# Output projection of block 1 ended by halves of the tokens, with the first half's norms beside it, and the norms' transposed tiles in four PSUM banks

## What is computed

```python
for l in range(DEPTH):
    h = rms_norm(x, mix_pre_gain[l])
    ... = split_columns(h @ w_in[l])
    ...                                   # 16 heads of four kinds of attention
    mixed = jnp.concatenate([o_a, o_b, o_c, o_d], axis=-1) @ w_out[l]
    x = x + rms_norm(mixed, mix_post_gain[l])
    h = rms_norm(x, ffn_pre_gain[l])
    y = conv_gated_mlp(h, w_up[l], conv_w[l], conv_b[l], w_down[l])
    x = x + rms_norm(y, ffn_post_gain[l])
```

## Time and profile before

| | us |
|---|---|
| median of three runs | 2374.84 |
| the profiled execution | 2370.15 |
| its span | 2368.4 |
| TensorE busy | 2066.8 |
| VectorE busy | 1739.2 |
| ScalarE busy | 841.7 |
| GpSimd busy | 698.6 |

### The profile page before, as it was taken

How to read it: one execution, slowest core, us unless ns; L and a number is a source line. 1 busy time by engine, 2 the same in 40 slices (tenths; PEclk the granted TensorE clock), 3 DMA queues, 4 the chain that set the end, 5 groups by cost and what they waited for, 6 DMA issues and landing times. The chain is left out here.

```text
span 2368.4 us, 27992 instructions
## 1 busy us (share of the span) xinstructions
PE 2066.8 (87%) x8693; PEld 1338.4 (57%) x8698; DVE 1739.2 (73%) x4197; ACT 841.7 (36%) x2074; POOL 698.6 (29%) x633
## 2 busy tenths in 40 slices
PE   7999999999979999998778788699899987777777
PEld 6779987779979775544233332297745543332222
DVE  6757777677767677778787877576677778787875
ACT  6656655666658611211111111277211211111110
POOL 1300001200001043444445434110343454444441
PEclk9999999999999889999989999999799999999999
DMA  6354532335545369999999999754499999999996
GB/s 221 110 179 179 186 136 83 135 125 186 186 145 164 125 236 419 420 421 421 422 421 421 421 421 421 272 158 152 167 420 419 422 421 421 421 421 421 421 421 270
DMA packets 138669, 700.53 MB, mean 296 GB/s; under 512 B 14392, under 2 KB 40248, under 8 KB 66872
## 3 DMA queue, kind: packets, MB, share of 16 engines
q0 software_dynamic: 73728, 536.90, 54.7%
q1 hardware_dynamic: 64824, 162.22, 19.6%
HBM read 698.03 MB, written 1.05 MB: 295 GB/s over the span
## 5 line engine op out<-in xcount | busy, mean ns | idle before, releaser
L2052 PE MATMUL bank<-ARENA 128*128 128x512 f32 x2048 | 989.8, 629 | 219.2 <-DVE ARENA L2354 217.8
L2052 PEld LDWEIGHTS bank<-ARENA 128*128 128x128 f32 x2048 | 385.1, 198 | 802.6 <-DVE ARENA L2354 431.7
L2344 DVE CUSTOM_DVE_ANT_0 ARENA<-ARENA 128x1024 f32<-128x1024 f32 x512 | 626.2, 1223 | 268.6 <-DMA ARENA<-in_uv_rows,ARENA 261.4
L1956 POOL DMA_INDIRECT ARENA<-in_uv_rows,ARENA x512 | 587.2, 1147 | 702.6 <-PE bank L2052 638.3
L154 PE MATMUL bank<-PARTS,PARTS 128*128 128x256 f32 (+4 forms) x1488 | 487.3, 327 | 12.6 <-DVE PARTS L284 5.9
L155 PE MATMUL bank<-PARTS,PARTS 128*128 128x256 f32 (+6 forms) x1552 | 496.3, 320 | 0.0
L156 PE MATMUL bank<-PARTS,PARTS 128*128 128x256 f32 (+6 forms) x1552 | 495.6, 319 | 0.0
L2160 ACT ACTIVATE ARENA<-ARENA 128x1 f32<-128x1 f32 x512 | 104.0, 203 | 1043.5 <-DVE ARENA L2344 1043.0
L155 PEld LDWEIGHTS bank<-PARTS,PARTS 128*128 128x128 f32 (+2 forms) x1552 | 297.8, 192 | 16.5 <-issue 1.0
L156 PEld LDWEIGHTS bank<-PARTS,PARTS 128*128 128x128 f32 (+2 forms) x1552 | 297.4, 192 | 16.8
L154 PEld LDWEIGHTS bank<-PARTS,PARTS 128*128 128x128 f32 x1488 | 285.9, 192 | 36.8 <-DVE PARTS L284 7.1
(11 more groups left out here) (262 smaller groups left out, 1900.3 us busy)
## 6 DMA issues: line engine op xcount, KB each, us to landing
ARENA<-in_w_up_tiles SPq DMA_DIRECT2D x44, 1024.0 KB, 6.7
ARENA<-in_w_down SPq DMA_DIRECT2D x44, 512.0 KB, 3.4
ARENA<-in_w_out SPq DMA_DIRECT2D x32, 512.0 KB, 4.2
ARENA<-in_wq_tiles SPq DMA_DIRECT2D x16, 1024.0 KB, 11.4
ARENA<-in_w_in SPq DMA_DIRECT2D x40, 384.0 KB, 3.8
ARENA<-in_w_in SPq DMA_DIRECT2D x24, 512.0 KB, 8.6
ARENA<-in_w_in SPq DMA_DIRECT2D x40, 256.0 KB, 2.8
ARENA<-in_uv_rows,ARENA POOLq DMA_INDIRECT x512
```

The source lines that it names most:

```text
L1956: nc.gpsimd.indirect_dma_start(out=slot[i % SLOTS], out_offset=None, in_=table[:, :], in_offset=bass.IndirectOffsetOnAxis(ap=picked[:, t, ...
L2052: last = mm(row_banks[t][n][:, :], diag[i % N_DIAG], slot[i % SLOTS][:, D + n * 512:D + (n + 1) * 512], start=(c == 0), stop=(c == NPICK - ...
L2344: v.tensor_tensor_reduce(u, u, xn[:, t, :], 1.0, 0.0, ALU.mult, ALU.add, dots[:, t, c:c + 1]).then_inc(S("dots_ready"), 1)
```

## The change

1. `post_norm` gets a mode `by_half`: its squares, gain products and roots can be issued one at a time, in the order of banks (0,0), (1,0), (0,1), (1,1), written as (t, n) with n the chunk; each waits for its own bank. VectorE takes a bank after ScalarE's square of it.

```diff
-            def act(act):
-                act.wait_ge(*done)
-                for t in range(NT):
...
+            order = [(t, n) for n in range(2) for t in range(NT)] if by_half else [(t, n) for t in range(NT) for n in range(2)]
+            squares_of = [order.index((t, 1)) + 1 for t in range(NT)]
+            def act(act, i):
+                t, n = order[i]
+                act.wait_ge(*done(t, n))
+                if n == 1 and not by_half:
+                    act.wait_ge(S(tag + "_scaled"), before + 2 * t + 1)
+                nc.scalar.activation(junk[:, 2 * t + n, :], out_bank[t][n][:, :], ACT.Square, scale=D ** -0.5,
+                                     accum_out=ss[:, 2 * t + n:2 * t + n + 1]).then_inc(S(tag + "_squares"), 1)
...
+            def scaled(dve, t, n):
+                if turn_waits(t, n):
+                    dve.wait_ge(*turn_waits(t, n))
+                cols = slice(n * 512, (n + 1) * 512)
+                nc.vector.tensor_tensor(mg[:, t, cols], out_bank[t][n][:, :], gain[:, cols], ALU.mult
+                                        ).then_inc(S(tag + "_scaled"), 1)
+            def turn_waits(t, n):
+                if by_half:
+                    return S(tag + "_squares"), before + order.index((t, n)) + 1
+                return (S(tag + "_squares"), before + 2 * t + 1) if n == 0 else done(t, n)
...
+                for t, n in ([(0, 0), (1, 0), (0, 1)] if by_half else [(0, 1), (0, 0), (1, 1), (1, 0)]):
+                    scaled(dve, t, n)
+            def dve_x(dve, t):
+                if by_half and t == 1:
+                    scaled(dve, 1, 1)
                 dve.drain()
-                for t in range(NT):
-                    dve.wait_ge(S(tag + "_rstd"), before_x + t + 1)
-                    nc.vector.scalar_tensor_tensor(X[:, t, :], mg[:, t, :], rstd[:, t:t + 1], X[:, t, :],
-                                                   ALU.mult, ALU.add).then_inc(S(tag + "_x"), 1)
```

```diff
+            def place(k):
+                return bank[4 + k // 4 * 2 + k % 2], k // 2 % 2 * T
...
+                    act.wait_ge(S(tag + "_turned"), before_k + ((2, 4, 4, 4)[k % 4] + k // 4 * 4))
+                    if k >= 2:
+                        act.wait_ge(S(tag + "_lo"), before_k + k - 1)
+                    to, at = place(k)
+                    nc.scalar.mul(HT_HI[:, k, :], to[:, at:at + T], gain(k)).then_inc(S(tag + "_hi"), 1)
...
+            def pe(pe, t):
+                pe.wait_ge(S(tag + "_xn"), before_t + t + 1)
+                for k in (0, 2, 1, 3, 4, 6, 5, 7):
+                    to, at = place(k)
+                    last = nc.tensor.transpose(to[:, at + t * P:at + (t + 1) * P], xn[:, t, k * P:(k + 1) * P], ident)
+                    if t == NT - 1:
+                        last.then_inc(S(tag + "_turned"), 1)
```

```diff
-                    return bank[4 + 2 * (c % 2) + t]
+                    return bank[t] if c == 0 else bank[4 + 2 * (c % 2) + t]
...
+                        if h >= NHD - 2:
+                            out.highs(act, KD + 2 * (h + 2 - NHD), KD + 2 * (h + 2 - NHD) + 2)
                     high_part(NHD // 2 - 1)
-                    out.highs(act, KD, out.n_units)
+                    out.highs(act, KD + 4, out.n_units)
...
-                            if n == KD:
-                                pe.wait_ge(s_("att_probsT"), NHD)
                             out.product(pe, n, out_bank)
+                    def projected_by_half():
+                        pe.wait_ge(s_("att_probsT"), NHD)
+                        for n in range(KD, out.n_units):
+                            last = out.half_product(pe, n, out_bank, 0)
+                        last.then_inc(s_("out_half"), 1)
+                        for n in range(KD, out.n_units):
+                            out.half_product(pe, n, out_bank, 1).then_inc(out.used(n)[0], 1)
...
-                            pe.wait_ge(S("norm_lo"), KD * 2 * l + max(2, k + 1))
+                            pe.wait_ge(S("norm_lo"), KD * 2 * l + k + 1)
```

4. The streams of `feeding(l)`:

```diff
+                projected = {(0, 0): out.used(KD), (1, 0): out.used(KD), (0, 1): mixed.out_half, (1, 1): out.done}
+                after_mix = post_norm(2 * l, lambda t, n: projected[t, n], out_bank, mix_post, f"mix_post_{l}", xn, junk,
+                                      by_half=True)
+                mid = pre_norm("norm", after_mix.x_ready, l, 1, xn, turn=2 * l + 1)
...
-                    after_ffn.pool(pool)
+                    for t in range(NT):
+                        after_mix.pool(pool, t)
+                        mid.pool(pool, t)
...
                 def act(act):
+                    for i in range(3):
+                        after_mix.act(act, i)
+                    mid.act_squares(act, 0)
                     up_down.act_early(act)
-                    after_mix.act(act)
-                    mid.act_squares(act)
+                    after_mix.act(act, 3)
+                    mid.act_squares(act, 1)
                     mid.act_high(act)
...
                 def dve(dve):
+                    after_mix.dve_scaled(dve)
+                    after_mix.dve_x(dve, 0)
+                    mid.dve_scale(dve, 0)
                     up_down.dve_early(dve)
-                    after_mix.dve(dve)
-                    mid.dve_scale(dve)
+                    after_mix.dve_x(dve, 1)
+                    mid.dve_scale(dve, 1)
                     mid.dve_low(dve)
                     up_down.dve(dve, following.lows if l + 1 < L else nothing)
...
                 def pe(pe):
                     up_down.pe_early(pe)
-                    keep_busy(32)
-                    mid.pe(pe)
+                    mid.pe(pe, 0)
+                    keep_busy(20, bank[0])
+                    mid.pe(pe, 1)
                     up_down.pe(pe)
                     if l + 1 < L:
                         keep_busy(32)
-                        pre.pe(pe)
+                        for t in range(NT):
+                            pre.pe(pe, t)
 
                 return stage(sp=sp, pool=pool, act=act, dve=dve, pe=pe)
```

More of the change, by code:

```diff
@@ L186, in stage, with keep_busy, post_norm @@
             return namedtuple("Stage", programs)(**programs)
-        def keep_busy(count):
+        def keep_busy(count, to=bank[7]):
             for _ in range(count):
-                nc.tensor.matmul(bank[7][:, :], ZERO[:, 0:P], ZERO[:, :], start=True, stop=True)
-        def post_norm(turn, done, out_bank, gain, gain_sem, mg, junk):
+                nc.tensor.matmul(to[:, :], ZERO[:, 0:P], ZERO[:, :], start=True, stop=True)
+        def post_norm(turn, done, out_bank, gain, gain_sem, mg, junk, by_half=False):
             tag = "post"
@@ L240, in read, with pre_norm @@
                 eng.wait_ge(S(tag + "_scaled"), before + 2 * NT)
-            return stage(act=act, pool=pool, dve=dve, banks_read=banks_read, read=read,
+            return stage(act=act, pool=pool, dve_scaled=dve_scaled, dve_x=dve_x, read=read,
                          x_ready=lambda t: (S(tag + "_x"), before_x + t + 1))
-        def pre_norm(tag, x_ready, l, which, xn, banks_read=None, first=4, turn=0):
+        def pre_norm(tag, x_ready, l, which, xn, turn=0):
             ss = STAT[:, 120:122]
@@ L1201, in _ @@
                     pool.drain()
-                    pre.pool(pool)
+                    for t in range(NT):
+                        pre.pool(pool, t)
                     for l in range(L):
@@ L1208, in _ @@
                 def _(act):
-                    pre.act_squares(act)
+                    for t in range(NT):
+                        pre.act_squares(act, t)
                     first.highs(act, 0, 6)
@@ L1220, in _ @@
                     nc.vector.memset(ZERO[:, :], 0.0)
-                    pre.dve_scale(dve)
+                    for t in range(NT):
+                        pre.dve_scale(dve, t)
                     first.lows(dve, 0, 6)
```

146 lines of the change are left out of this document (65 added, 81 removed).

## The result

The changed kernel takes 2379.57 us (median of 20 runs, 2376.19 to 2381.39) against 2375.1 of the kernel before (20 runs, 2370.26 to 2377.14). The ratio is 1.0016, with a 95% interval of 1.001 to 1.0022: slower, by 4 us (4.5 between the medians), just inside the 0.2% that I had called no change, and inside my range (2369.5 to 2380.5). The forecast was 2375.7.

What follows compares the result with a forecast made beforehand. The norm chain on VectorE, ScalarE and GpSimd before block 1's FFNs was taken to bound the kernel there, while TensorE waits. Terms +2.0 - 1.45 + 0.3 = +0.9 on a median of 2374.84 gave 2375.7 us, range 2369.5 to 2380.5.

Steps and rivals of the forecast that it cites:

- The half order delivers the first half early, and the weight split takes its place: Block 1, before the FFN: first scale near 139, split ending near 145.8, second transposes +0.35 us per layer.
- GpSimd held up by the split: Second half's norm, block 1: VectorE's weight split may delay GpSimd's root from 145.0 to 146.5, costing 0 to +0.2 us.
- the 0.9 that it would have added: Upper-bound case before the FFN: GpSimd holds up VectorE's weight split, up to 0.9 us more per layer.
- Tiles in four banks, +0.8 in layer 0: FFN's first product waits for three low parts instead of two: +0.8 us in layer 0, +0.5 in layer 1.
- Both parts together, +2.0 forecast: Block 1, both layers: the tiles in four banks plus 0.35 per layer for the second transposes, 1.15 + 0.85 = +2.0 us.
- Input projections, -1.45: Four input projections: the first product waits for one low part instead of two, -1.45 us in all, bounds 0 and -2.
- The clock, +0.3: FFN's first product: clock falls and likely returns 3.4 us behind the second transposes; +0.3 us both layers, bounds -0.9 and +3.2.
- the slower rival: FFN's first product, both layers: clock returns late, 157.8 in layer 0; +3.8 us in all, 2378.6 us; chance 0.15.
- the term that the prediction had summed along VectorE's queue: Block 1, before the FFN: second transposes later by +0.35 us per layer, bounds -0.3 and +1.5.

Runs made afterwards that it cites:

- spread split: Changed kernel with the FFN's early weight split cut in three and placed between the second half's steps on ScalarE and VectorE; ratio to the kernel before 0.9989.
- seven banks: Spread split with 33 fillers, and the eight transposed tiles in front of the FFN in seven banks instead of four; ratio to the kernel before 0.9962.
- 44 fillers: Changed kernel with 44 instead of 20 filler matmuls between the two halves' transposes before each FFN of block 1; ratio to the kernel before 1.0001.
- old streams: Changed kernel with the earlier instruction order: weight split ahead of the norms, 32 fillers ahead of all 16 transposes; ratio to the kernel before 0.9994.
- only four banks: Kernel before with only the norms' transposed tiles put in four banks, streams and projection order unchanged; ratio to the kernel before 1.0013.
- the hole was filled: Changed kernel with two more fillers behind the second half's transposes, before the FFN's first product; ratio to the kernel before 1.0008.

## Why the prediction was right, and where it was off

1. *The half order delivers the first half early, and the weight split takes its place.* Right to 0.4 us at each step: first scale 138.69 (139.0), split's end 145.4 (145.8), second scale 149.91 (150.3 less the handovers; 150.0 to 150.5 was announced), first product 153.66 (153.7). Shown by the spread split: move the split and 3.2 us per layer go.
2. *Bounds: GpSimd held up by the split.* Right: 2.16 for 0.31, 0.3 us late for X. The Trainium skill ("SBUF — State Buffer", section "SBUF: two separate sides") says that whichever of the two starts first has the shared port pair for its whole instruction, and the other is blocked. This trace agrees that GpSimd is the one held up, but it was held up for longer than one instruction: VectorE started three more of its split (143.58, 144.18, 144.78) before GpSimd's ended. In the other direction, GpSimd stretching VectorE's split, this trace doesn't show it (4.90 against 4.91), so the 0.9 that it would have added wasn't there.
3. *Tiles in four banks, +0.8 in layer 0.* Right, 0.80 at full clock; seven banks gave 0.66 and 0.22 of it back. Both parts together, +2.0 forecast: 15.36 less 13.96 and 14.23 make +2.5; with the clock up in both kernels it is +2.3 (15.11 less 13.94 and 13.96), so 0.2 of it is the clock and 0.3 is layer 1, where the tiles cost 0.8 as well and not 0.5.
4. *Input projections, -1.45.* A little too much: -(0.1 + 0.29 + 0.39 + 0.39) = -1.2. At the program's start the product stands behind the split of the first weights, and these came 0.4 us later from the DMA than in the kernel before, in the second execution 0.7 later.
5. *The clock, +0.3.* This term was mis-sized, and it is nearly the whole difference between forecast and result. The units lost 1.68 and 1.89 more than before: +3.6. I had taken the return from two earlier ones, 3.4 us behind the fall; it came 10.2 us behind it. And I had the fall at the second transposes (151.0); it came 1.2 us ahead of them, at 149.5. I had 3.2 as upper bound and the late return as the slower rival (2378.6, at 0.15), so the result lies at that rival, not at the forecast; the clock came back even later than in that rival (159.7, not 157.8). What I didn't see was that the change makes a second hole, of 1 us, between transposes and product; the old kernel had none. So the figure is inside the range because the range reached to the late return, and inside the 0.2% by 0.3 us: that part is luck.

   I weighed the rule of the Trainium skill ("TensorE: Matmul & The Clock Gate", Part 1) that the window runs freely, so that the return would move between executions; the page puts the movement at about half a microsecond. In front of the FFN the two executions of each kernel agree with that: the low stretch was as long to 0.1 us, and the fall moved by 0.1 us (changed) and 0.2 us (before). There the difference between 3.4 and 10.2 belonged to the kernel and not to chance. Elsewhere the executions differed by more, and the rule is borne out: in block 2's second layer 10.2 against 6.8 us for the same kernel, twice; and the first 139 us of the program are the same with 20 and with 44 fillers, but only the second had the clock low there, from 14.3 on for 3.4 us.
6. *The order within `post_norm`.* The prediction didn't see it as a gain of its own; the kernel with the old streams has 0.6 us per layer from it, since ScalarE's squares no longer wait for VectorE's gain products. At full clock the chain adds up: 13.95 + 0.8 for the tiles - 0.6 + 0.94 for the new streams = 15.1. The last two make +0.35 together, which is just the term that the prediction had summed along VectorE's queue.

Sum: +2.5 - 1.2 + 3.6 = +4.9, against +5.3 and +4.6 at the first products of block 2's two layers (704.10 less 698.80, 1542.48 less 1537.89) and +4.5 between the medians.

Open: why the clock sometimes does not fall. After 3.17 us of idle time it fell in both layers of both executions of the kernel before and in layer 1 of the kernel with only four banks, but not in layer 0 of that one; after 2.57 us (old streams) it fell in layer 0 and not in layer 1.

How long it stays low can be put in an order, found only afterwards and tested by no run of its own. Take the start of the transposes that end the idle time, and the hole between the transposes and the first product. Of the 14 low stretches in front of the FFN, four lasted 3.4 us: the clock fell when these transposes had begun (or in the same 0.1 us), and there was no hole. Five lasted 6.8: either there was the hole, and the fall came behind that start or at most 0.5 us ahead of it (old streams, split spread), or the hole was filled and the fall came 1.0 to 1.4 us ahead. Five lasted 10.2, those with both: the fall 1.0 to 2.5 us ahead, and the hole. So a hole of 1 us doesn't by itself make the stretch 10.2 us long. What decides where in the idle time the clock falls stays open.

## What to carry to other kernels

A chain that is split into halves gains only if the second half's chain starts when its data are there; look at what the in-order queue of the busiest helper (here VectorE) does between the two halves, and put independent work there in pieces, at the places where that engine waits. Price the clock with the change's own idle times, all of them, the ones just after work resumes too: with the same 3.2 us idle ahead, the first unit lost 1.9 us where such a hole followed and 0 to 0.9 where none did. Idle TensorE time in front of a serial stage is cheap to fill; it gave back 3.6 us in the changed kernel, and nothing that the runs can show in the kernel before.

## What the runs showed that I had not expected

- A 0.98 us hole between 2 us of transposes and the next product: the clock stayed at 1.2 GHz for 10.2 us after its fall with it, 6.8 without it, at the same 5.8 us of idle time ahead (two executions with it, one without).
- In front of the FFN the low stretch was as long in a second execution of each kernel, in both layers; in front of block 2's last input projection it was 6.8 us in one execution and 10.2 in the other, of both kernels.
- The same idle time (3.17 us, and 2.57) let the clock fall in some layers and not in others.
- A GpSimd instruction of 0.31 us, begun under VectorE's weight split, ended only behind it, after 2.16 us; VectorE's instructions kept their length.
